# Turning the normalised activations between sublayers: a scaled copy and plain transposes in place of a product with a diagonal

## The chip, the cores and the metric

The kernel runs on one NeuronCore of a Trainium2 chip. The metric is the device time of one execution in microseconds (us). TensorE does the matrix products, VectorE, ScalarE and GpSimd work on tiles, SyncE issues the DMAs. In the rows they are PE (PEld its weight loads), DVE, ACT, POOL and SP.

## The reference

One step of a two-layer backbone over 512 latent and 128 context tokens, width 1024, all in float32. Each layer has three sublayers, FFN, mixing, FFN; each takes a normalised and modulated copy of the running tokens `x` and adds its gated result to it:

```python
def rmsnorm(x, g):
    y = xf * lax.rsqrt(jnp.mean(xf * xf, axis=-1, keepdims=True) + EPS)
    return (y * g.astype(jnp.float32)).astype(x.dtype)

def modulate_in(x, g_pre, mod, j):
    return rmsnorm(x, g_pre) * (1.0 + mod[:, :, 3 * j + 1]) + mod[:, :, 3 * j]

def gated_residual(x, out, g_post, mod, j, weight):
    return x + weight * mod[:, :, 3 * j + 2] * rmsnorm(out, g_post)
```

The mixing is neighbourhood attention and mLSTM heads in layer 0, a gated short convolution in layer 1. The products are done as three products of rounded high and low parts (`hT_hi`, `hT_lo`, `w_hi`, `w_lo`), 320 or 512 columns each.

## The kernel before

The 640 tokens are five tiles of 128 (`NT` = 5), held in SBUF for the whole run as `X`, tokens on the partitions, 1024 columns a tile. The six sublayers (`SUBS`) follow one another; `boundary(s)` of ScalarE and VectorE, the tile loops of GpSimd and `turn_x(s)` of TensorE are the stretch between sublayer s-1 and s. Each engine runs its own instructions in program order, and semaphores tie them together. No scheduler has a part in it: the order is that of the code.

For each tile the boundary does this, the steps of one tile interleaved with those of its neighbours:

- VectorE evacuates the output sums from PSUM (`evac`, L1267), gates the second half (L1245), and adds the result to `X` (`add_out`, L1250) once GpSimd has the factor of the output's norm (`post_r`, L1119 and L1120).
- ScalarE squares the new tile and sums it (`square_x`, L920).
- GpSimd makes the row factor 1/rms of it (`pre_r`: L1103, L1104) and multiplies it into a diagonal 128x128 matrix (L1127). Two diagonals exist. GpSimd's order is post_r(q), pre_r(q-1), for q = 0 to 5.
- TensorE turns the tile: eight float32 products with a slice of `X` as the stationary operand and the diagonal as the moving one (L607), which scales the rows and puts the features on the partitions. They go to one of two PSUM areas `TR` (banks 6 and 7, or 4 and 5).
- ScalarE modulates, which is a scale and a bias per feature (`modulate`, L930, eight activations), and VectorE splits the result into high and low parts (`split_h`, L1255 and L1256).

`first_units` then starts the next sublayer's products (L614): the first half of the columns needs tiles 0 to 2, the second half all five (`hT_ready`). They come after all of `turn_x` in TensorE's order. The first boundary (s = 0) has no output to add. ScalarE splits the second weight tile after modulating tile 3, VectorE after splitting tile 3.

Of the kernel before, what the change touches and what calls it, by code (L numbers as in the profile page):

```python
# [20 lines left out]
ALU = mybir.AluOpType  # L21
ACT = mybir.ActivationFunctionType
AX = mybir.AxisListType
P = 128

D = 1024
LAT, CTX = 512, 128
TOK = LAT + CTX
NT = TOK // P
CT = LAT // P  # L30
KD = D // P
# [89 lines left out]
def build(nc, x_prompt, x_sample, cache_k, cache_v, state_C, state_n, state_m, c, c_ctx, ada_w,  # L121
# [4 lines left out]
    with ctx:  # L126
        sb = lambda name, shape, dt=F32: ctx.enter_context(nc.sbuf_tensor(name, shape, dt))
        sem = lambda name: ctx.enter_context(nc.semaphore(name))
        at = lambda name, shape, off, dt=F32: nc.alloc_sbuf_tensor_at(name, shape, dt, offset=off)
# [4 lines left out]
        end = nc.sbuf_usable_end  # L134
        o = base

        def take(name, shape, dt=F32):
            nonlocal o
            t = at(name, shape, o, dt)
            size = 4  # L140
            for w in shape[1:]:
                size *= w
            where[name] = o
            o += (size + 31) // 32 * 32
            return t

        where = {}
        X = take("x", [P, NT, D])
# [10 lines left out]
        ident = take("ident", [P, P])  # L159
# [5 lines left out]
        ssq = take("mean_sq", [P, 3, NT])  # L165
        msq = take("mean_sq_eps", [P, 3, NT])
        rms = take("rms", [P, 2, NT])
        diag = take("diag", [P, 2, P])
        ones = take("ones", [P, 1])
        halfneg = take("minus_half", [P, 20])  # L170
        ccol = take("cond_cols", [P, 2, KD])
# [16 lines left out]
        assert conv_at + 2 * (TOK + 16) * 4 <= end  # L188

        h_mod = at("h_mod", [P, 2, KD, P], arena)  # L190

        ada0 = at("ada_first", [P, PRO, KD, MODW], arena)
        adab0 = at("ada_bias_first", [2, PRO * MODW], where["part"])
# [59 lines left out]
        TR = [flat(pair(6)).rearrange("p (k t) -> p k t", t=P), flat(pair(4)).rearrange("p (k t) -> p k t", t=P)]  # L253
# [12 lines left out]
        act_ready, out_ready, out_evac = sem("act_ready"), sem("out_ready"), sem("out_evac")  # L266
        ssq_post, r_post, x_new = sem("ssq_post"), sem("r_post"), sem("x_new")
        ssq_half, gated_half, gated = sem("ssq_half"), sem("gated_half"), sem("gated")
        ssq_pre, diag_ok, xT_ok = sem("ssq_pre"), sem("diag_ok"), sem("xT_ok")
        hmod_ok, hT_ready = sem("hmod_ok"), sem("hT_ready")  # L270
        s_dve, s_pool = sem("s_dve"), sem("s_pool")
        s_ident, s_const, s_slow, s_x, s_c = sem("s_ident"), sem("s_const"), sem("s_slow"), sem("s_x"), sem("s_c")
# [289 lines left out]
        def _(pe):  # L562
            mm = nc.tensor.matmul
# [3 lines left out]
            for i in range(PRO):  # L567
                for k in range(KD):
                    if k % (KD // 2) == 0:
                        pe.wait_ge(first_loaded[i][k // (KD // 2)], 16)  # L570
                    last = mm(PS[0:2, i, :], csil[:, :, k], ada0[:, i, k, :], start=(k == 0), stop=(k == KD - 1))
# [4 lines left out]
            for kind in range(2):  # L576
                for k in range(KD):
                    col = (kind * KD + k) * 2
                    last = nc.tensor.transpose(PS[:, 0, col:col + 2], flat(mrow0[:])[:, kind * D + k:(kind + 1) * D:KD], ident[0:2, 0:2])
# [15 lines left out]
            def turn_x(s):  # L595

                if s == 0:
                    pe.wait_ge(s_x, 32)
                    pe.wait_ge(neg_ok, 2)
                for t in range(NT):  # L600
                    pe.wait_ge(diag_ok, NT * s + t + 1)
                    if s and t < 2:
                        pe.wait_ge(out_evac, plan[s][0]["oe"] - (0 if t else NT))
                    if t >= 2:
                        pe.wait_ge(hmod_ok, NT * s + t - 1)
                    for k in range(KD):
                        last = mm(TR[t % 2][:, k, :], X[:, t, k::KD], diag[:, t % 2, :], start=True, stop=True)  # L607
                    last.then_inc(xT_ok, 1)

            def unit_half(p, h, width=P):  # L610
# [483 lines left out]
        @block.gpsimd  # L1094
        def _(pool):
            own = Steps(pool, s_pool)
            pool.memset(halfneg[:], -0.5).then_inc(neg_ok, 1)
            pool.memset(ones[:], 1.0).then_inc(neg_ok, 1)
            pool.wait_ge(neg_ok, 2)
            pool.wait_ge(s_ident, 16)  # L1100

            def rsqrt(dst, tmp, src, width, scale):
                own.link(pool.tensor_scalar(tmp, src, scale, EPS, ALU.mult, ALU.add))  # L1103
                return pool.tensor_tensor(dst, tmp, halfneg[:, 0:width], ALU.pow)  # L1104

            def gate_first_half(s, t):

                pool.wait_ge(ssq_half, NT * s + t + 1)
                if t == 0:
                    pool.wait_ge(gate_ready, s + 1)  # L1110
                if s:
                    pool.wait_ge(r_post, NT * s)
                pool.tensor_scalar(msq[:, 0, t:t + 1], ssq[:, 0, t:t + 1], EPS, None, ALU.add)  # L1113
                pool.tensor_tensor(part[:, t, 0:512], part[:, t, 0:512], G[:, cond(t), 0:512], ALU.mult).then_inc(gated_half, 1)

            def post_r(s, t):
                pool.wait_ge(ssq_post, NT * s + t + 1)
                pool.wait_ge(gated_half, NT * (s + 1))
                own.link(pool.tensor_tensor(msq[:, 1, t:t + 1], ssq[:, 1, t:t + 1], msq[:, 0, t:t + 1], ALU.add))  # L1119
                pool.tensor_tensor(rms[:, 1, t:t + 1], msq[:, 1, t:t + 1], halfneg[:, 0:1], ALU.pow).then_inc(r_post, 1)  # L1120

            def pre_r(s, t):
                pool.wait_ge(ssq_pre, NT * s + t + 1)
                own.link(rsqrt(rms[:, 0, t:t + 1], msq[:, 2, t:t + 1], ssq[:, 2, t:t + 1], 1, 1.0))
                if t >= 2:
                    pool.wait_ge(xT_ok, NT * s + t - 1)
                pool.tensor_scalar(diag[:, t % 2, :], ident[:], rms[:, 0, t:t + 1], None, ALU.mult).then_inc(diag_ok, 1)  # L1127

            for s, kind in enumerate(SUBS):
                for q in range(NT + 1):  # L1130
                    if s and q < NT:
                        post_r(s - 1, q)
                    if q:
                        pre_r(s, q - 1)
                if kind == "sc":
                    pool.wait_ge(hT_ready, NT * (s + 1))
                    pool.memset(upad[:], 0.0).then_inc(conv_zero, 1)
                if kind == "ab":
                    pool.wait_ge(hT_ready, NT * (s + 1))
                    pool.memset(padsb[:], 0.0).then_inc(pad_zero, 1)  # L1140
                    pool.memset(vmt[:, :, :, MLD:MLD + 1], 1.0).then_inc(ones_ok, 1)
                    pool.wait_ge(ones_ok, 1)
                    nv, nd = 0, 0
                    whole = [z[1] for q, z in enumerate(ML_STEPS) if z[1] in [y[1] for y in ML_STEPS[:q]]]

                    def head_r(n):
                        pool.wait_ge(h_ssq_ok, n + 1)
                        c4 = slice(whole[n] * MLH, (whole[n] + 1) * MLH)
                        rsqrt(hr[:, c4], hms[:, c4], hssq[:, c4], MLH, 1.0 / MLD).then_inc(h_r_ok, 1)

                    for q, (dr, cc) in enumerate(ML_STEPS):
                        edge = P - 1 if dr == 0 else 0
                        if cc < CT:
                            pool.wait_ge(ml_wi, q + 1)
                            if q >= 2:
                                pool.wait_ge(ml_num, q - 1)
                            pool.tensor_tensor(qs[:, q % 2], FT[:, 8:12, cc * P:(cc + 1) * P], wi[:, q % 2], ALU.mult).then_inc(ml_qs, 1)
                        if q in NEEDS_STATE:
                            pool.wait_ge(ml_w, q + 1)
                            if nv >= 2:  # L1160
                                pool.wait_ge(ml_c, nv - 1)
                            wl = Wx[:, q % 2, :, edge:edge + 1].to_broadcast([P, MLH, MLD + 1])
                            pool.tensor_tensor(vw[:, nv % 2], vmt[:, cc], wl, ALU.mult).then_inc(ml_vw, 1)
                            nv += 1
                        if cc in [z[1] for z in ML_STEPS[:q]]:
                            nd += 1
                            if nd >= 2:
                                head_r(nd - 2)
                    head_r(NT - 1)
                for t in range(NT):  # L1170
                    gate_first_half(s, t)
            for t in range(NT):
                post_r(len(SUBS) - 1, t)
# [515 lines left out]
```

## Time and profile before

| what | value |
|---|---|
| median of 3 runs | 3026.76 us (3025.64 to 3029.79) |
| span of the profiled execution | 3024.5 us |
| TensorE matmul busy | 2856.1 us (94%) |
| VectorE busy | 1460.8 us (48%) |
| ScalarE busy | 676.4 us (22%) |
| GpSimd busy | 188.8 us (6%) |
| mean granted clock of TensorE | 0.938 of full |
| L607, the turning products | 480 rows, 117.6 us busy |
| TensorE waiting for L1127 before L607 | 44.8 us |

The span reaches from the first instruction to the last; the page has no second figure for the profiled execution's time, so the span stands beside the runs. A float32 product appears as two rows of TensorE, two passes each. Rows of one engine that overlap are pipelined: the spacing of starts is what a product costs in a row of them, not its own length.

### The profile page before, as it was taken

Reading aid. Unit: us, or ns where it says so; the run is one execution under the profiler, and the core shown is the slowest. Engines: PE = TensorE matmul, PEld = TensorE weight load, DVE = VectorE, ACT = ScalarE, POOL = GpSimd, SP = SyncE. Lnnn points to the kernel's source line nnn. Section 1 sums busy time; section 2 is a strip of 40 time slices with the busy share of each in tenths; the row PEclk is TensorE's granted clock in tenths of the full one; section 3 lists DMA queues with packets and bytes.
Section 4 is the critical chain, followed back from the end, with each engine's and each line's share of the span. In section 5 each row is a group of like instructions: output and inputs, shape, how many; then the busy total and the mean of one; then the engine's idle time right before and its main releaser. Section 6 shows DMA issues by size and latency. Waiting matters only on the chain.

```text
span 3024.5 us, 42142 instructions
## 1 busy us (share of the span) xinstructions
PE 2856.1 (94%) x15952; PEld 2551.4 (84%) x15952; DVE 1460.8 (48%) x2590; ACT 676.4 (22%) x1192; POOL 188.8 (6%) x245
## 2 busy tenths in 40 slices
PE   8999999799979978899999989999999998999998
PEld 5997898599857766798899779889979998998996
DVE  2774774622155554675477367633334444322333
ACT  3111111322122121411111241111123114111212
POOL 1000000400000021200000120000012003000002
PEclk9999999999955578999999989999999999999999
DMA  5443443222510003343344224332221221222222
GB/s 198 139 125 105 139 139 119 77 70 70 94 37 19 7 7 88 92 138 97 112 138 150 81 86 138 107 94 76 87 80 50 77 87 54 75 66 84 73 87 87
DMA packets 384157, 276.06 MB, mean 91 GB/s; under 512 B 48224, under 2 KB 349728, under 8 KB 384052
## 3 DMA queue, kind: packets, MB, share of 16 engines
q1 hardware_dynamic: 384054, 274.67, 30.8%
q8 instruction: 67, 1.10, 0.2%
q14 instruction: 36, 0.29, 0.0%
HBM read 266.88 MB, written 7.71 MB: 91 GB/s over the span
## 4 chain that ended last, share of the span: by engine, by line
PE 56%; DVE 3%; POOL 1%; ACT 1%; issue 1%; DMA 0%; POOLq 0%; ACTq 0%; DVEq 0%
PE psum L645 35%; PE psum L591 6%; PE psum L592 6%; PE psum L593 6%; PE psum L614 2%; PE psum L607 2%; PE psum L587 1%; DVE w_lo L1225 1%; DVE mod_acc L1203 0%; ACT w_hi L897 0%; DVE part L1269 0%; DVE part L1267 0%; POOL rms L1104 0%; DVE gate L1241 0%; ACT h_mod L930 0%
## 5 line engine op out<-in xcount | busy, mean ns | idle before, releaser
L1225 DVE TENSOR_TENSOR w_lo<-w_raw,w_hi 128x1024 fp32r<-128x1024 f32 (+1 forms) x437 | 423.9, 970 | 1016.1 <-ACT w_hi L897 1010.9
L645 PE MATMUL psum<-hT_hi,w_hi 128*128 128x320 f32 (+1 forms) x3472 | 799.3, 311 | 4.2 <-DVE part L1269 4.2
L645 PE MATMUL psum<-hT_lo,w_hi 128*128 128x320 f32 (+1 forms) x3472 | 793.0, 310 | 0.0
L645 PE MATMUL psum<-hT_hi,w_lo 128*128 128x320 f32 (+1 forms) x3472 | 792.7, 309 | 0.0
L897 ACT ACTIVATE w_hi<-w_raw 128x1024 fp32r<-128x1024 f32 (+1 forms) x437 | 372.3, 852 | 1225.9 <-PE psum L593 537.8
L645 PEld LDWEIGHTS psum<-hT_hi,w_hi 128*128 128x128 f32 (+1 forms) x3472 | 579.3, 188 | 51.8 <-issue 45.1
L645 PEld LDWEIGHTS psum<-hT_lo,w_hi 128*128 128x128 f32 (+1 forms) x3472 | 581.3, 188 | 0.8
L645 PEld LDWEIGHTS psum<-hT_hi,w_lo 128*128 128x128 f32 (+1 forms) x3472 | 581.0, 188 | 0.8
L591 PE MATMUL psum<-w_hi,act_hi 128*128 128x512 f32 x960 | 382.9, 399 | 17.8 <-DVE mod_row L1214 9.7
L592 PE MATMUL psum<-w_lo,act_hi 128*128 128x512 f32 x960 | 380.2, 396 | 0.0
L593 PE MATMUL psum<-w_hi,act_lo 128*128 128x512 f32 x960 | 380.1, 396 | 0.0
L1203 DVE SCALAR_TENSOR_TENSOR mod_acc<-ada_raw,cond_silu,mod_acc 128x256 f32<-128x256 f32 x896 | 371.0, 482 | 0.0
L591 PEld LDWEIGHTS psum<-w_hi,act_hi 128*128 128x128 f32 x960 | 180.8, 188 | 78.7 <-DVE mod_row L1214 14.4
L593 PEld LDWEIGHTS psum<-w_hi,act_lo 128*128 128x128 f32 x960 | 180.8, 188 | 43.7
L592 PEld LDWEIGHTS psum<-w_lo,act_hi 128*128 128x128 f32 x960 | 180.7, 188 | 42.3
L968 ACT ACTIVATE silu_g<-psum 128x640 f32<-128x640 f32 x88 | 61.9, 704 | 613.8 <-PE psum L645 584.5
L1331 DVE TENSOR_TENSOR u_tmp<-psum,silu_g 128x640 f32<-128x640 f32 x88 | 72.6, 825 | 197.2 <-PE psum L645 195.8
L607 PE MATMUL psum<-diag,x 128*128 128x128 f32 x480 | 117.6, 420 | 44.8 <-POOL diag L1127 44.8
L607 PEld LDWEIGHTS psum<-diag,x 128*128 128x128 f32 x480 | 115.5, 335 | 47.9 <-POOL diag L1127 47.2
L1113 POOL TENSOR_SCALAR mean_sq_eps<-mean_sq 128x1 f32<-128x1 f32 x30 | 10.8, 360 | 2144.6 <-ACT junk L909 2144.4
L930 ACT ACTIVATE h_mod<-psum,mod_cols 128x128 f32<-128x128 f32 x240 | 87.7, 498 | 18.0 <-PE psum L607 18.0
L1314 DVE TENSOR_TENSOR act_lo<-u_tmp,act_hi 128x640 f32 (+1 forms) x96 | 79.3, 826 | 10.0
(170 smaller groups left out, 2034.8 us busy)
## 6 DMA issues: line engine op xcount, KB each, us to landing
w_raw<-in_ffn_w_dram SPq DMA_DIRECT2D x176, 512.0 KB, 4.1
ada_raw<-in_ada_w_dram SPq DMA_DIRECT2D x128, 512.0 KB, 3.6
w_raw<-in_ffn_w_dram SPq DMA_DIRECT2D x176, 256.0 KB, 2.6
w_raw<-in_ab_w_in_dram SPq DMA_DIRECT2D x28, 512.0 KB, 4.0
w_raw<-in_sc_w_in_dram SPq DMA_DIRECT2D x24, 512.0 KB, 4.0
ada_first<-in_ada_w_dram SPq DMA_DIRECT2D x8, 1024.0 KB, 12.6
gate<-modulation SPq DMA_DIRECT2D x6, 1024.0 KB, 6.1
w_raw<-in_ab_w_out_dram SPq DMA_DIRECT2D x16, 256.0 KB, 2.8
```

The lines of the kernel that those rows point to most:

```text
L591: mm(out, a_hi, b_hi, start=first, stop=False)
L592: mm(out, a_hi, b_lo, start=False, stop=False)
L593: return mm(out, a_lo, b_hi, start=False, stop=final)
L607: last = mm(TR[t % 2][:, k, :], X[:, t, k::KD], diag[:, t % 2, :], start=True, stop=True)
L645: last = mm(IN[p][0:width, h, 0:HT], a, b[:, k, h * HT:(h + 1) * HT], start=(k == 0 and a is hi and b is hT_hi), stop=(k == KD - 1 and a i ...
L897: A(dst, src, ACT.Copy).then_inc(w_hi_ok, 1)
L930: last = A(h_mod[:, t % 2, k, :], TR[t % 2][:, k, :], ACT.Identity, scale=mcol[:, s % 2, 1, cond(t), k:k + 1], bias=mcol[:, s % 2, 0, cond ...
L968: A(halves(sg[:]), IN_V[nb % 2], ACT.Silu).then_inc(in_evac[nb % 2], 1)
L1203: ins = V.scalar_tensor_tensor(acc[:, cd, :], w, col, acc[:, cd, :], ALU.mult, ALU.add)
L1225: V.tensor_tensor(d_, a, b.bitcast(F32), ALU.subtract).then_inc(w_lo_ok, 1)
L1314: V.tensor_tensor(lo, src, hi.bitcast(F32), ALU.subtract).then_inc(act_ready, 1)
L1331: V.tensor_tensor(halves(ut[:]), IN_V[p], halves(sg[:]), ALU.mult).then_inc(in_evac[p], 1)
```

## The change

The diagonals go. GpSimd multiplies the whole tile of `X` by its row factor into a new buffer `x_norm` of three tiles at the end of SBUF, and TensorE turns it with transposes against the identity matrix. The products' operands `X` and the diagonal are replaced; semaphore `diag_ok` becomes `xn_ok`; GpSimd may now run three tiles ahead of TensorE in place of two.

```diff
-        diag = take("diag", [P, 2, P])
...
+        xn = at("x_norm", [P, 3, D], (end - 3 * D * 4) // 32 * 32)
...
                 for t in range(NT):
-                    pe.wait_ge(diag_ok, NT * s + t + 1)
+                    pe.wait_ge(xn_ok, NT * s + t + 1)
...
                     for k in range(KD):
-                        last = mm(TR[t % 2][:, k, :], X[:, t, k::KD], diag[:, t % 2, :], start=True, stop=True)
+                        last = nc.tensor.transpose(TR[t % 2][:, k, :], xn[:, t % 3, k::KD], ident[:])
...
-                if t >= 2:
-                    pool.wait_ge(xT_ok, NT * s + t - 1)
-                pool.tensor_scalar(diag[:, t % 2, :], ident[:], rms[:, 0, t:t + 1], None, ALU.mult).then_inc(diag_ok, 1)
+                if t >= 3:
+                    pool.wait_ge(xT_ok, NT * s + t - 2)
+                pool.tensor_scalar(xn[:, t % 3, :], X[:, t, :], rms[:, 0, t:t + 1], None, ALU.mult).then_inc(xn_ok, 1)
```

## Rows read from the trace of the kernel before

**Rows 1.** The page, part 4: share of the chain that ended last, by line

```profile
PE psum L645 35%; PE psum L591 6%; PE psum L592 6%; PE psum L593 6%; PE psum L614 2%; PE psum L607 2%; PE psum L587 1%; DVE w_lo L1225 1%; DVE mod_acc L1203 0%; ACT w_hi L897 0%; DVE part L1269 0%; DVE part L1267 0%; POOL rms L1104 0%; DVE gate L1241 0%; ACT h_mod L930 0%
```

**Rows 2.** Timeline, TensorE, 2262:2291; start us, us, engine, line, operation, count, [idle before]

```profile
2270.49 11.74 PE L607 MATMUL psum<-diag,x 128*128 128x128 f32 x48 [7.37 <-POOL diag L1127]
2283.12 7.90 PE L607 MATMUL psum<-diag,x 128*128 128x128 f32 x32 [0.89 <-POOL diag L1127]
2290.77 0.39 PE L614 MATMUL psum<-hT_hi,w_hi 128*128 128x320 f32 x1
```

**Rows 3.** Timeline, GpSimd, 2263:2286

```profile
2267.48 0.19 POOL L1103 TENSOR_SCALAR mean_sq_eps<-mean_sq 128x1 f32<-128x1 f32 x1 [0.86 <-ACT part L920]
...
2269.25 1.18 POOL L1127 TENSOR_SCALAR diag<-ident,rms 128x128 f32<-128x128 f32 x1
...
2276.99 0.61 POOL L1127 TENSOR_SCALAR diag<-ident,rms 128x128 f32<-128x128 f32 x1
2278.20 0.19 POOL L1119 TENSOR_TENSOR mean_sq_eps<-mean_sq,mean_sq_eps 128x1 f32<-128x1 f32 x1 [0.61 <-ACT junk L909]
...
2284.74 0.61 POOL L1127 TENSOR_SCALAR diag<-ident,rms 128x128 f32<-128x128 f32 x1
```

**Rows 4.** Timeline, VectorE, 2255:2302

```profile
2269.26 0.68 DVE L1245 TENSOR_TENSOR part<-part,gate 128x512 f32<-128x512 f32 x1
...
2286.54 1.22 DVE L1256 TENSOR_TENSOR hT_lo<-h_mod,hT_hi 128x1024 fp32r<-128x1024 f32 x1
```

**Rows 5.** Timeline, TensorE, 1049:1056: transposes in the mixing stage

```profile
1049.28 2.40 PE L791 MATMUL psum<-ident,attn_tok 128*128 128x128 f32 x10
```

**Rows 6.** Timeline, TensorE, 680:683: transposes between weight products

```profile
680.27 0.71 PE L699 MATMUL psum<-ident,feat_tmp 128*128 128x128 f32 x5
```

**Rows 7.** Groups by line and form, GpSimd; busy us, mean ns, idle before

```profile
L1114 POOL TENSOR_TENSOR part<-part,gate 128x512 f32<-128x512 f32 x30 | 39.4, 1314 | 1.9
...
L1163 POOL TENSOR_TENSOR v_weighted<-vm_tok,decay 128x516 f32<-128x516 f32 x8 | 8.4, 1051 | 10.8 <-ACT decay L1076 10.8
...
L1137 POOL MEMSET u_pad<- 128x643 f32 x1 | 0.6, 636 | 10.7 <-DVE hT_lo L1256 10.7
...
L1097 POOL MEMSET minus_half<- 128x20 f32 x1 | 0.1, 114 | 0.3 <-POOLq L1677 0.3
```

**Rows 8.** Timelines, GpSimd and VectorE, 1056:1100: the mLSTM stage

```profile
1063.34 1.06 POOL L1163 TENSOR_TENSOR v_weighted<-vm_tok,decay 128x516 f32<-128x516 f32 x1
...
1064.10 0.85 DVE L1558 TENSOR_TENSOR decay<-decay,mlmask 128x512 f32<-128x512 f32 x1
```

**Rows 9.** Stretches; busy of each engine (x instructions), granted clock, DMA share, GB/s

```profile
853.00:1040.00 187.00, 186.41 (x626) 142.04 (x627) 100.84 (x307) 40.12 (x144) 0.00 (x0) 0.50 0.07 15
1049.00:1055.00 6.00, 4.93 (x22) 4.10 (x22) 4.15 (x6) 0.00 (x0) 0.00 (x0) 0.50 0.00 0
2274.00:2282.00 8.00, 8.00 (x35) 8.00 (x34) 5.11 (x6) 7.39 (x21) 6.70 (x11) 1.00 0.00 0
2285.00:2287.00 2.00, 2.00 (x10) 2.00 (x10) 1.16 (x2) 0.78 (x3) 0.35 (x1) 0.50 0.00 0
```

**Rows 10.** Timeline, TensorE, 1156:1162: first products after the mLSTM stage

```profile
1157.06 0.63 PE L592 MATMUL psum<-w_lo,hT_hi 128*128 128x512 f32 x1
...
1160.90 0.52 PE L592 MATMUL psum<-w_lo,hT_hi 128*128 128x512 f32 x1
1161.26 0.39 PE L593 MATMUL psum<-w_hi,hT_lo 128*128 128x512 f32 x1
...
1161.73 0.39 PE L592 MATMUL psum<-w_lo,hT_hi 128*128 128x512 f32 x1
```

**Rows 11.** Timelines, TensorE 39:60 and GpSimd 0:60: the first boundary

```profile
40.08 19.29 PE L607 MATMUL psum<-diag,x 128*128 128x128 f32 x80 [0.72 <-POOL diag L1127]
59.13 0.39 PE L614 MATMUL psum<-hT_hi,w_hi 128*128 128x320 f32 x1
...
53.78 0.61 POOL L1127 TENSOR_SCALAR diag<-ident,rms 128x128 f32<-128x128 f32 x1
```

More of the change, by code:

```diff
@@ L268, in build @@
         ssq_half, gated_half, gated = sem("ssq_half"), sem("gated_half"), sem("gated")
-        ssq_pre, diag_ok, xT_ok = sem("ssq_pre"), sem("diag_ok"), sem("xT_ok")
+        ssq_pre, xn_ok, xT_ok = sem("ssq_pre"), sem("xn_ok"), sem("xT_ok")
         hmod_ok, hT_ready = sem("hmod_ok"), sem("hT_ready")
```

## The prediction

> **What bounds the kernel now.** I read the chain of waits first. TensorE holds it: the biggest piece is the weight products of L645, and the turning products of L607 hold 2% [rows 1]. The change touches only L607 and what feeds it, so the place to read is the stretch between two sublayers, of which there are six. I take the one at 2263 to 2291 us as the pattern; those at 580, 1214, 1748 and 2517 us have the same shape, and from the first turning product to the first unit the same length within 0.15 us. The timeline of TensorE there [rows 2] shows three turned tiles in 11.74 us, a wait of 0.89 us for GpSimd, two more tiles, and the first unit's product at 2290.77. From 2283.12 to 2290.77 are two tiles, 3.83 us each (16 passes of float32). Everything after 2290.77 follows TensorE, so a boundary is worth what that one start moves.
>
> The next question is how far behind TensorE the others are. GpSimd's timeline [rows 3] runs from 2267.48 to 2285.35 (2284.74 + 0.61) with one wait of 0.61 us between two of its instructions; the small rows that are not shown fill the rest without gaps. It makes its last diagonal only 5.42 us before the first unit begins. **GpSimd is nearly a second bound**, hidden by one and a half tiles of TensorE. The first three tiles' high and low parts, which the first products need, are ready at 2287.76 (2286.54 + 1.22) [rows 4], so that wait ends 3 us before it matters.
>
> **TensorE's part.** Each tile's 8 float32 products (16 passes) become 8 transposes. The trace has transposes of the same shape, 128x128 float32 against the identity: 10 in 2.40 us at half the full clock [rows 5] and 5 in 0.71 us at the full clock [rows 6]. A single one's own length is included in each, so the spacing is about 0.225 and 0.11 us, and 8 take 2.0 us or 1.05 us. I take 2.0, because TensorE will work in short bursts (next part but one). Per tile 1.8 us of 3.83 go. But of five tiles only the last one lies on the path after GpSimd's last row: the others vanish in waits for GpSimd. Their 7 us are worth nothing here.
>
> **GpSimd's part.** Five times per boundary the multiplication of 128 columns becomes one of 1024. Undisturbed it took 0.61 us before [rows 3]. No row has 1024 columns on this engine, so I bound it from slopes [rows 7]:
> - lowest: memsets of 20 and of 643 columns took 0.114 and 0.636 us, 0.84 ns a column, and 0.61 + 896 x 0.84 ns = 1.36 us.
> - the product with one streamed operand and one that is spread from a single column, 516 columns, 1.05 us: less 0.19 for the shortest instruction, 1.67 ns a column, and 0.61 + 896 x 1.67 ns = 2.11 us.
> - the product of two streamed operands, 512 columns, 1.31 us: 2.2 ns, so 2.58 us.
> - highest: 0.19 us for 1 column against 0.61 for 128 [rows 3] is 3.3 ns a column, so 3.57 us.
> I take 2.11 us: it is the row with the same kind of operands, one streamed tile times one value per partition. The ends stay for the range. The Trainium skill's page "GPSIMD Engine Reference", section "When to use GPSIMD", says otherwise: there such one-input work goes at roughly the line rate and only two-input work is about twice as slow as on VectorE (where it advises elementwise work to go). A line rate is what the memset row shows; the sum by it is the first rival.
>
> The five rows together grow by 5 x (2.11 - 0.61) = 7.5 us. Nothing covers them: GpSimd does not idle there, and its next r for the residual stands behind each scaling, so the addition to x of the later tiles, the square on ScalarE and again GpSimd's next factor all slide. The last scaling ends at 2285.35 + 7.5 = 2292.85, and 2.0 us of transposes end at 2294.9. The first unit starts 4.1 us later than 2290.77. Both the wait of 0.61 us, which may be absorbed, and the new collisions work on this figure, in opposite directions.
>
> **The collisions.** A GpSimd instruction that starts while VectorE works on two SBUF operands waits for it: a diagonal started at 2269.25 took 1.18 us instead of 0.61, and VectorE's gating product ran from 2269.26 for 0.68 us [rows 3, 4]. It works the other way as well: in the mLSTM stage VectorE's addition at 1064.10 took 0.85 us instead of 0.69 beside a GpSimd product that ended at 1064.40 [rows 8]. With scalings of 2 us VectorE will wait up to 2 us at some of its additions and splits. I price it at zero to 1 us per boundary and leave it to the range, since VectorE has gaps of 1 to 2 us there.
>
> **The clock.** Before, TensorE is busy from 2270.49 on with one short break, and its granted clock is 1.00 at 2274 to 2282, 0.50 (1.2 GHz) for a moment at 2285 to 2287, and full (2.4 GHz) again when the units begin [rows 9]; the turning products were as long at either level, so it cost nothing. In the new form TensorE idles 7 us and more, then works 2 us in every 5. In the stretch with bursts of transposes and short products, 853 to 1040 us, and in 1049 to 1055, the clock was 0.50 throughout [rows 9]. I expect 0.50 when the first unit begins. What that costs is seen after the mLSTM stage: dense products started at 1156.5, spaced 0.427 us until 1160.90 and 0.235 from 1161.26 on [rows 10]: ten products that each lose 0.19, **2.0 us** in 4.4 us. The same 4.4 us of half clock cost the L614 products the same share. That is 2.0 us for each of the five boundaries. Nothing covers it, TensorE having no slack from there on.
>
> **The first boundary** (at 40 us) has no residual ahead of it. There TensorE ran 19 us without a break and GpSimd waited for it; its last diagonal ran at 53.78, the first unit started at 59.13 [rows 11]. With 2.11 us in place of 0.61 that last scaling ends at 55.9, or 57.2 if it must wait for a split of VectorE, and the transposes at 57.9 to 59.2. That is 0 to 1.2 us earlier, against 0 to 2 us of clock: I count nothing.
>
> **The sum.** 5 x (4.1 + 2.0) + 0 = 30.5 us. The profiled span is 3024.5 us; the runs' median of 3026.76 is 2.3 us longer, which I take as work outside the span that stays. 3024.5 + 30.5 = 3055 of span, **3057 us** as a time.
>
> **The rivals.**
> 1. GpSimd at the memset's rate, 1.36 us. Then the last scaling ends at 2285.35 + 3.75 = 2289.1, the transposes at 2291.1, 0.3 us late. With the clock's 2.0 this gives 5 x 2.3 = 11.5 us, 3038; with a full clock 1.5 us, 3028. For it: nothing but the memset's slope. Against it: the 516-column row, and the 0.42 us that 127 more columns added to the smallest row of the same kind. Chance 0.15 (0.10 with little or none of the clock's loss, 0.05 with it). What the page says of one-input work is this rival.
> 2. **Faster.** The freed 1.8 us of TensorE's tile comes through. The point from which it decides is the length of a scaling: 2285.35 + 5 x (S - 0.61) + 2.0 = 2290.77 gives S = 1.29 us. At 1.1 us and with a full clock (transposes in 1.05 us) the units would start 1.9 us earlier, of which some 1.5 remain since the second weight tile's low part is not ready before; five times that and some 3 us at the first boundary, where each step waits for TensorE and the first tile would be done at 39.9 + 1.1 + 1.1 instead of 40.1 + 3.8, is 10.5 us: 3016. For it: TensorE was the last to finish in every boundary. Against it: 1.1 us is below all four bounds. Chance 0.11.
> 3. The scaling at the highest slope, 3.57 us, or at 2.58 with VectorE's additions waiting behind it. Late by 5 x 2.96 - 3.42 (5.42 less the 2.0 us of transposes) = 11.4 us, with the clock 13.4, five times 67 us, and the first boundary loses about 8: 3102; at 2.58 it is 5 x (6.4 + 2.0) = 42, 3069. Chance 0.14 for over 3075.
> 4. The forecast, a scaling of 1.7 to 2.6 us with a cold or half-cold clock: 3045 to 3070. Chance 0.60.
> That the change would not do what it says can be set aside: the diff leaves no diagonal, and both engines' instructions at L607 and L1127 are replaced one by one, none added.
>
> **How the numbers follow.** The range of 3026 to 3090 leaves out the faster case and the far end of rival 3, and holds rival 1 nearly whole. About 0.2% (6 us) is what a measurement of this kernel can tell from no change. Faster by more than that: rival 2, 0.11. Within: rival 1 without the full loss, 0.10. Slower: 0.60 + 0.14 + 0.05 = 0.79.
>
> **What the new profile would show.** The group of L1127 on GpSimd near 2.1 us undisturbed, up to 2.9 beside VectorE; TensorE's waits for it grown from 44.8 us to over 80 and spread over nearly every tile; L607 with 240 rows in place of 480 and about 55 us busy; the first L614 product of the pattern boundary some 4 us later after the last product before it; a granted clock of 0.50 at that product and a spacing near 0.27 us for about 4 us. A scaling below 1.3 us, or a full clock at the first unit, would make the prediction wrong.

## The result and the profile after

| | before | changed |
|---|---|---|
| median of the runs on this chip | 3026.2 us (4 runs, 3025.5 to 3029.8) | 3076.86 us (4 runs, 3075.4 to 3078.7) |
| ratio to before | 1 | 1.0163 (95% interval 1.0149 to 1.0178) |
| profiled span | 3024.5 us | 3073.6 us, +49.1 |
| mean granted clock of TensorE | 0.938 | 0.918 |
| TensorE waiting for L1127 before L607 | 44.8 us | 146.4 us |
| GpSimd busy | 188.8 us | 263.3 us, +74.5 |

The change makes the kernel 1.6% slower, some 50 us. The prediction said 3057 us with a range of 3026 to 3090; the direction and the place were right, the size was short by 20 us.

The page of the changed kernel, first the busy times of part 1, then the chain of part 4 (compare [rows 1]; this chain was followed back only over 15% of the span, so its shares can't be set beside the old ones):

```profile
PE 2802.3 (91%) x15712; PEld 2489.7 (81%) x15712; DVE 1465.6 (48%) x2590; ACT 677.5 (22%) x1192; POOL 263.3 (9%) x245
...
PE psum L645 10%; PE psum L591 2%; PE psum L593 2%; PE psum L592 2%; PE psum L614 0%; DVE part L1267 0%; DVE x L1250 0%; DVE w_lo L1225 0%; DVE gate L1241 0%; PE psum L607 0%; POOL mean_sq_eps L1119 0%; DVE part L1269 0%; ACT w_hi L897 0%; ACT junk L909 0%; DVE part L1245 0%; POOLq L126 0%
```

TensorE does 54 us less work and the kernel is 49 us longer. The groups by line (busy us, mean ns of one, then idle before and its releaser) say where the waiting is:

```profile
L607 PE MATMUL psum<-ident,x_norm 128*128 128x128 f32 x240 | 59.1, 426 | 146.4 <-POOL x_norm L1127 146.4
```

```profile
L1127 POOL TENSOR_SCALAR x_norm<-x,rms 128x1024 f32<-128x1024 f32 x30 | 103.2, 3439 | 3.1
```

```profile
L1250 DVE SCALAR_TENSOR_TENSOR x<-part,rms,x 128x1024 f32<-128x1024 f32 x30 | 38.6, 1286 | 57.3 <-POOL rms L1120 57.0
```

TensorE's wait grew by 102 us, more than the 58.5 us of turning work that went. One scaling costs 3.44 us on average, where the prediction took 2.11. VectorE's addition of the residual, L1250, waits 57 us for GpSimd's row factor (20 before).

The pattern boundary on TensorE, as in [rows 2] (start us, us, line, count, idle before). Here the last product ahead of it starts at 2292.13:

```profile
2302.14 1.97 PE L607 MATMUL psum<-ident,x_norm 128*128 128x128 f32 x8 [9.61 <-POOL x_norm L1127]
2308.23 1.97 PE L607 MATMUL psum<-ident,x_norm 128*128 128x128 f32 x8 [4.13 <-POOL x_norm L1127]
2315.52 1.97 PE L607 MATMUL psum<-ident,x_norm 128*128 128x128 f32 x8 [5.31 <-POOL x_norm L1127]
2322.28 1.97 PE L607 MATMUL psum<-ident,x_norm 128*128 128x128 f32 x8 [4.79 <-POOL x_norm L1127]
2327.46 1.97 PE L607 MATMUL psum<-ident,x_norm 128*128 128x128 f32 x8 [3.21 <-POOL x_norm L1127]
2329.09 0.62 PE L614 MATMUL psum<-hT_hi,w_hi 128*128 128x320 f32 x1
2329.50 0.47 PE L614 MATMUL psum<-hT_lo,w_hi 128*128 128x320 f32 x1
...
2331.97 0.31 PE L614 MATMUL psum<-hT_hi,w_lo 128*128 128x320 f32 x1
```

Every tile is waited for, 3.2 to 5.3 us each, and each is turned in 1.97 us. Before, the first unit's product came 27.66 us after the end of the last weight product; now it comes 36.57 us after it, 8.9 us later. In the five boundaries it is 7.1, 8.8, 8.8, 8.9 and 8.8 us later, 42.3 us in all. That is most of the 49.1.

GpSimd in the same stretch, as in [rows 3]:

```profile
2296.89 0.19 POOL L1103 TENSOR_SCALAR mean_sq_eps<-mean_sq 128x1 f32<-128x1 f32 x1 [0.86 <-ACT part L920]
...
2298.66 3.42 POOL L1127 TENSOR_SCALAR x_norm<-x,rms 128x1024 f32<-128x1024 f32 x1
...
2304.78 3.40 POOL L1127 TENSOR_SCALAR x_norm<-x,rms 128x1024 f32<-128x1024 f32 x1
...
2309.33 1.67 POOL L1104 TENSOR_TENSOR rms<-mean_sq_eps,minus_half 128x1 f32<-128x1 f32 x1
2311.11 4.36 POOL L1127 TENSOR_SCALAR x_norm<-x,rms 128x1024 f32<-128x1024 f32 x1
...
2318.39 3.84 POOL L1127 TENSOR_SCALAR x_norm<-x,rms 128x1024 f32<-128x1024 f32 x1
...
2324.56 2.85 POOL L1127 TENSOR_SCALAR x_norm<-x,rms 128x1024 f32<-128x1024 f32 x1
```

It works without a gap from 2296.89 to 2327.41, and the first unit starts 1.68 us after that: the last tile's transposes start at 2327.46, and the unit's product follows in the spacing of starts, 1.63 us later (1.97 us is the length of the row, with the last transpose's own end in it). The last scaling, with nothing beside it, takes 2.85 us; the other four take 3.40 to 4.36. VectorE shows why, as in [rows 4]:

```profile
2298.68 0.67 DVE L1245 TENSOR_TENSOR part<-part,gate 128x512 f32<-128x512 f32 x1
2302.98 1.28 DVE L1250 SCALAR_TENSOR_TENSOR x<-part,rms,x 128x1024 f32<-128x1024 f32 x1 [3.63 <-POOL rms L1120]
...
2311.00 1.23 DVE L1256 TENSOR_TENSOR hT_lo<-h_mod,hT_hi 128x1024 fp32r<-128x1024 f32 x1
2312.14 0.68 DVE L1245 TENSOR_TENSOR part<-part,gate 128x512 f32<-128x512 f32 x1
...
2318.28 1.23 DVE L1256 TENSOR_TENSOR hT_lo<-h_mod,hT_hi 128x1024 fp32r<-128x1024 f32 x1
2321.65 1.13 DVE L1255 CAST hT_hi<-h_mod 128x1024 fp32r<-128x1024 f32 x1 [2.14 <-ACT h_mod L930]
```

The scaling issued at 2311.11 has VectorE's subtraction (two SBUF operands) in front of it from 2311.00, and the gating product right behind that, until 2312.82; it lasts 1.51 us longer than the undisturbed one. The one at 2304.78 meets one product of 0.68 and lasts 0.55 longer. Where the scaling is in front, VectorE pays: the cast at 2321.65 takes 1.13 in place of 0.69 us. GpSimd's small steps are lengthened as well: L1104 takes 0.57 us where nothing is beside it (at 2284.07 in the kernel before) and 1.39 to 1.67 us in all five tiles here. But in the kernel before four of five took 1.40 to 1.56, and all small steps together grow by only 0.1 us in this boundary, so this is no part of the loss.

The clock, by stretches as in [rows 9]:

```profile
2302.00:2308.00 6.00, 1.97 (x8) 1.57 (x8) 2.48 (x3) 3.70 (x10) 5.65 (x6) 0.50 0.00 0
2327.00:2329.00 2.00, 1.54 (x7) 1.54 (x8) 1.74 (x2) 1.14 (x2) 0.41 (x1) 0.50 0.00 0
2329.00:2331.00 2.00, 2.00 (x10) 2.00 (x9) 1.35 (x2) 1.52 (x5) 0.00 (x0) 0.50 0.00 0
2331.00:2333.00 2.00, 2.00 (x14) 2.00 (x13) 0.59 (x1) 1.38 (x4) 0.00 (x0) 0.83 0.55 146
2333.00:2336.00 3.00, 3.00 (x23) 3.00 (x22) 1.33 (x2) 0.00 (x0) 0.63 (x1) 1.00 0.26 78
```

The first unit meets a granted clock of 0.50 (1.2 GHz), and in the TensorE rows above its products start 0.267 us apart until 2331.6 and 0.147 from then on. Over what a unit loses before too, that adds 1.14 us in the first boundary and 0.51, 0.52, 0.57, 1.16 and 0.84 in the others.

The first boundary, as in [rows 11]:

```profile
57.64 1.97 PE L607 MATMUL psum<-ident,x_norm 128*128 128x128 f32 x8 [1.90 <-POOL x_norm L1127]
59.26 0.61 PE L614 MATMUL psum<-hT_hi,w_hi 128*128 128x320 f32 x1
```

```profile
54.73 2.85 POOL L1127 TENSOR_SCALAR x_norm<-x,rms 128x1024 f32<-128x1024 f32 x1
```

Its first unit starts at 59.26 in place of 59.13. GpSimd is the bound there too now, and ends just as late as TensorE had. The clock's 1.14 us does not arrive: the stretch from this unit to the next boundary's last weight product is only 0.1 us longer than before.

The account of 49.1 us, from the ends of the weight products and the starts of the units: 42.3 us in the five boundaries, 0.1 in the first, 3.6 of slow first products in the five, and 3.1 left over. This rest lies in the stretch between the second and the third boundary (608.12 us in place of 604.42, of which 0.5 is clock), where the wait of L739 for VectorE is 14.8 us in place of 12.9. The same stretch was 605.0 to 607.4 us long in the experiments, in no order with what they change, so the changed kernel's is the longest of all; its cause stays open.

### The profile page after: what moved, and what is told of

Its sections match the earlier page's. It is cut to its first block and busy times, and to the rows that moved or that the text cites. A ratio compares the mean times of both kernels' runs of the same rounds, so it can differ in the third digit from the quotient of the medians.

```text
span 3073.6 us, 41656 instructions
## 1 busy us (share of the span) xinstructions
PE 2802.3 (91%) x15712; PEld 2489.7 (81%) x15712; DVE 1465.6 (48%) x2590; ACT 677.5 (22%) x1192; POOL 263.3 (9%) x245
## 5 line engine op out<-in xcount | busy, mean ns | idle before, releaser
L592 PEld LDWEIGHTS psum<-w_lo,act_hi 128*128 128x128 f32 x960 | 181.0, 189 | 42.4
L607 PE MATMUL psum<-ident,x_norm 128*128 128x128 f32 x240 | 59.1, 426 | 146.4 <-POOL x_norm L1127 146.4
L607 PEld LDWEIGHTS psum<-ident,x_norm 128*128 128x128 f32 x240 | 47.1, 220 | 158.3 <-POOL x_norm L1127 155.2
L1127 POOL TENSOR_SCALAR x_norm<-x,rms 128x1024 f32<-128x1024 f32 x30 | 103.2, 3439 | 3.1
L930 ACT ACTIVATE h_mod<-psum,mod_cols 128x128 f32<-128x128 f32 x240 | 86.7, 465 | 26.1 <-PE psum L607 26.0
```

The source lines that it names most:

```text
L592: mm(out, a_hi, b_lo, start=False, stop=False)
L607: last = nc.tensor.transpose(TR[t % 2][:, k, :], xn[:, t % 3, k::KD], ident[:])
L930: last = A(h_mod[:, t % 2, k, :], TR[t % 2][:, k, :], ACT.Identity, scale=mcol[:, s % 2, 1, cond(t), k:k + 1], bias=mcol[:, s % 2, 0, cond ...
L1127: pool.tensor_scalar(xn[:, t % 3, :], X[:, t, :], rms[:, 0, t:t + 1], None, ALU.mult).then_inc(xn_ok, 1)
```

## The experiments

Two theories stand at the start. Theory A is the prediction's, with GpSimd's length corrected: the boundary is as long as GpSimd's chain, and a first unit is later by the growth of five scalings less TensorE's old lead of 3.4 us; the clock is a small second term. Rivals put the loss on the transposes, on the cold clock, or on the waits between VectorE and GpSimd.

### 1 and 2. The scaling cut to 128 and to 512 columns

The tile is turned from x itself, so the scaling of the rows is missing from these kernels' results; from one to the other only the length of GpSimd's instruction changes.

```diff
-                        last = nc.tensor.transpose(TR[t % 2][:, k, :], xn[:, t % 3, k::KD], ident[:])
+                        last = nc.tensor.transpose(TR[t % 2][:, k, :], X[:, t, k::KD], ident[:])
...
-                pool.tensor_scalar(xn[:, t % 3, :], X[:, t, :], rms[:, 0, t:t + 1], None, ALU.mult).then_inc(xn_ok, 1)
+                pool.tensor_scalar(xn[:, t % 3, 0:128], X[:, t, 0:128], rms[:, 0, t:t + 1], None, ALU.mult).then_inc(xn_ok, 1)
```

The second has 0:512 in place of 0:128.

> The transposes stay, but GpSimd scales only the first 128 columns of a tile (0.61 us, as the diagonal took), and TensorE turns x itself. The scaling of the rows is left out. Theory A, GpSimd's chain sets the start of the next sublayer: 5 x 2.24 us of scaling and its collisions go from each boundary, the first unit starts up to 3.4 us earlier than in the kernel before in boundaries 1 to 5 (2 to 2.5 us of it kept, the second weight tile's low part being next), about 4 us earlier in the first, less 0.5 to 1.2 us of clock each: a span of 3010 to 3018 us against 3024.5 before. Theory B, the short bursts of transposes and the half clock behind them are the cost: it stays over 3050.

> As e1, with 512 columns scaled. The line through 0.61 us for 128 and 2.85 us for 1024 columns gives 1.57 us for a scaling. Theory A: the first unit is 5 x 0.96 - 3.42 = 1.4 us later than before in boundaries 1 to 5, and with 0.8 us of clock each and 1.5 us gained at the first the span is about 3034 us (3030 to 3040). If not a line but a threshold is behind the loss (one scaling shorter than TensorE's old tile of 3.8 us is hidden), this kernel is as fast as e1.

128 columns: 3011.85 us, ratio 0.9947 (0.9931 to 0.9964), span 3010.8, **13.7 us faster than before**. 512 columns: 3041.7 us, ratio 1.0047 (1.0030 to 1.0064), span 3042.4. Both kernels' L1127 groups, and from the second a scaling in the first boundary, where nothing is beside it:

```profile
L1127 POOL TENSOR_SCALAR x_norm<-x,rms 128x128 f32<-128x128 f32 x30 | 37.4, 1246 | 3.1
```

```profile
L1127 POOL TENSOR_SCALAR x_norm<-x,rms 128x512 f32<-128x512 f32 x30 | 70.2, 2341 | 3.1
```

```profile
41.68 1.57 POOL L1127 TENSOR_SCALAR x_norm<-x,rms 128x512 f32<-128x512 f32 x1
```

So an undisturbed scaling takes 0.61, 1.57 and 2.85 us at 128, 512 and 1024 columns: exactly 2.5 ns per column on top of 0.29 us. The transposes are the same in all three kernels, which clears them: with short scalings they win 13.7 us. In the last four boundaries first units come 2.6 to 2.7 us later than before at 512 columns, 1.3 in the first of the five (the prediction's formula, 5 x (1.57 - 0.61) - 3.42, gives 1.4; in the pattern boundary the five scalings together run 4.6 us over their undisturbed length, 1.6 before), and 3.0 to 3.9 us earlier at 128 columns (formula: 3.42 earlier). The first was inside its expectation, the second some 2 us above: the formula holds to about 1 us per boundary, collisions come on top. A straight line between the two spans crosses 3024.5 at 1.03 us of scaling, about 300 columns; the prediction put the break-even of the first units at 1.29 us, with no loss of clock behind them.

### 3. The change with float32 products in place of the transposes

```diff
-                        last = nc.tensor.transpose(TR[t % 2][:, k, :], xn[:, t % 3, k::KD], ident[:])
+                        last = mm(TR[t % 2][:, k, :], xn[:, t % 3, k::KD], ident[:], start=True, stop=True)
```

> The changed kernel, with float32 products against the identity in place of the transposes, so GpSimd's 1024 columns alone are left of the change; computes all. Theory A: of TensorE's five tiles only the last lies behind GpSimd's last row, so it is 1.9 us slower than the changed kernel in each of the six boundaries, less what a higher clock gives back (up to 0.8 each): a span of 3079 to 3086 us against 3073.6. Theory B, the transposes' bursts cost through the clock: it is faster than the changed kernel by 5 us or more.

3085.28 us, ratio 1.0191 (1.0174 to 1.0208), span 3083.8. As expected: the last tile's products are on the path behind GpSimd, and the first units come 2.1 to 2.3 us later than in the changed kernel (3.7 in the first boundary): a tile of products takes 3.85 us up to the first unit's start there, the transposes 1.63. The transposes by themselves are worth about 10 us even where GpSimd is late (10.2 by the spans, 0.28% by the ratios).

### 4. The changed kernel with products in TensorE's waits

Before each turned tile of boundaries 1 to 5, TensorE runs products whose results are not used (24 before the first tile, 8 before each other).

```diff
+                    if s:
+                        if t == 0:
+                            pe.wait_ge(w_lo_ok, plan[s][0]["nin"] + 1)
+                            pe.wait_ge(out_evac, plan[s][0]["oe"] - NT)
+                        p = plan[s][0]["nin"] % 2
+                        for _ in range(24 if t == 0 else 8):
+                            mm(PS[:, 0, :], w_hi[:, p, 0, :], w_hi[:, p, 0:4, :].rearrange("p a b -> p (a b)"), start=True, stop=True)
```

> The changed kernel, with products nobody reads put into TensorE's idle time of boundaries 1 to 5: 24 of 512 columns before the first tile, 8 before each other, so that the clock stays up. Theory A: only what the trace of the changed kernel shows as slow first products comes back, 0.5 to 1.2 us per boundary and 0.9 us of each boundary's last transposes, together 5 to 8 us: a span of 3066 to 3069 us. Theory B: most of the 49 us comes back, under 3045.

3069.18 us, ratio 1.0147 (1.0130 to 1.0164), span 3065.9, 7.7 us under the changed kernel's; by the ratios the gain is 0.16%, and their intervals overlap. The number is where it was expected, but the trace backs only part of it. The first units come 0.2 to 0.7 us earlier (2.3 us in five boundaries, the last transposes being quicker). The slow first products vanish in boundaries 1 and 3 but not in 2, 4 and 5, where they lose 1.1, 1.4 and 1.1 us: 3.6 us in all, as much as without the fillers. Here is the fourth: its third, fourth and fifth tile (the added lines make L607 into L614 and L1127 into L1134), and stretches around its first unit, which starts at 2321.15:

```profile
2308.16 1.97 PE L614 MATMUL psum<-ident,x_norm 128*128 128x128 f32 x8 [4.30 <-POOL x_norm L1134]
...
2314.92 1.16 PE L614 MATMUL psum<-ident,x_norm 128*128 128x128 f32 x8 [1.38 <-POOL x_norm L1134]
...
2320.11 1.39 PE L614 MATMUL psum<-ident,x_norm 128*128 128x128 f32 x8 [2.18 <-POOL x_norm L1134]
```

```profile
2316.00:2320.00 4.00, 1.93 (x9) 1.24 (x7) 1.62 (x2) 3.85 (x9) 3.90 (x2) 1.00 0.00 0
2320.00:2323.00 3.00, 2.89 (x15) 2.89 (x16) 2.96 (x3) 1.46 (x5) 0.06 (x1) 0.65 0.00 0
2323.00:2326.00 3.00, 3.00 (x18) 3.00 (x17) 1.49 (x2) 1.44 (x5) 0.00 (x0) 0.78 0.51 140
```

The fillers don't fill the waits: TensorE still idled 4.30, 1.38 and 2.18 us before the third, fourth and fifth tile. The granted clock was 1.00 at 2316 to 2320, where TensorE was busy 1.93 of 4 us, and then 0.65 and 0.78, where it was busy nearly all the time. So this run does not show what a TensorE that never idles would be granted. Of the rest of the 7.7 us, 3.1 lie in the stretch between the second and the third boundary, 0.5 of them slow products and the others the length that scatters in all kernels. What these fillers gave back by quicker transposes and products is 2 to 3 us of the 49. The rival that most of the loss is the clock's falls; a full clock at the first unit is not had reliably by these fillers.

### 5. The scaling on VectorE

GpSimd keeps the row factor and hands it over; VectorE scales behind its addition for the tile after. Transposes as in the change.

```diff
-                own.link(rsqrt(rms[:, 0, t:t + 1], msq[:, 2, t:t + 1], ssq[:, 2, t:t + 1], 1, 1.0))
-                if t >= 3:
-                    pool.wait_ge(xT_ok, NT * s + t - 2)
-                pool.tensor_scalar(xn[:, t % 3, :], X[:, t, :], rms[:, 0, t:t + 1], None, ALU.mult).then_inc(xn_ok, 1)
+                rsqrt(rms[:, 0, t:t + 1], msq[:, 2, t:t + 1], ssq[:, 2, t:t + 1], 1, 1.0).then_inc(r_pre, 1)
...
+            def scale_x(s, t):
+                dve.wait_ge(r_pre, NT * s + t + 1)
+                if t >= 3:
+                    dve.wait_ge(xT_ok, NT * s + t - 2)
+                V.tensor_scalar(xn[:, t % 3, :], X[:, t, :], rms[:, 0, t:t + 1], None, ALU.mult).then_inc(xn_ok, 1)
...
+                    if 2 <= q < NT + 2 and s < len(SUBS):
+                        scale_x(s, q - 2)
```

> The scaling goes from GpSimd to VectorE, behind its addition to the tile after (x_norm of tile q - 2 after add_out of tile q - 1); the transposes stay; computes all. VectorE's cast of 1024 columns took 0.69 us, so a scaling should take 0.7 (1.2 if it runs at one column a cycle). Theory A: GpSimd's chain loses even the diagonal, so TensorE's 1.8 us per tile finally count: the first unit starts 2 to 3.4 us earlier than before in boundaries 1 to 5, 3 to 4 us in the first, less 0.5 to 1.2 us of clock each: a span of 3010 to 3017 us, faster than both kernels. Rival: VectorE's own order (it now waits for GpSimd's factor with additions and splits queued behind it) takes what it gives, and the span is 3022 to 3035 us.

3013.06 us against 3030.27 of the kernel before on that chip, ratio 0.9946 (0.9932 to 0.9959), span 3008.9. **It computes everything and beats both kernels**: 0.5% faster than before, 2.1% faster than the change as it was made. The VectorE group and, from the pattern boundary, ScalarE's and TensorE's rows at its end:

```profile
L1253 DVE TENSOR_SCALAR x_norm<-x,rms 128x1024 f32<-128x1024 f32 x30 | 22.6, 752 | 11.1 <-POOL rms L1104 11.0
```

```profile
2271.46 5.67 ACT L930 ACTIVATE h_mod<-psum,mod_cols 128x128 f32<-128x128 f32 x16
```

```profile
2271.09 1.97 PE L607 MATMUL psum<-ident,x_norm 128*128 128x128 f32 x8 [2.48 <-DVE x_norm L1253]
2274.48 1.94 PE L607 MATMUL psum<-ident,x_norm 128*128 128x128 f32 x8 [1.42 <-ACT h_mod L930]
2276.42 0.60 PE L614 MATMUL psum<-hT_hi,w_hi 128*128 128x320 f32 x1
```

The same 1024 columns that take GpSimd 2.85 us take VectorE 0.75. The first units come 3.6 to 3.8 us earlier than before, 4.4 in the first boundary. GpSimd's part of the chain is no longer last, if only just: the fifth tile waits for ScalarE's modulated copies (h_mod, L930), which run back to back, and its scaling on VectorE had ended 0.38 us before the transposes start (2274.10 and 2274.48). Of 22.8 us won at the first units, 7.8 are given back by slower first products (0.75 to 2.1 us in each boundary where before had 0.3); TensorE still works in bursts.

### 6. The same with products in TensorE's waits

The fillers of run 4 (4 in place of 8 before the later tiles) on top of run 5.

> e4 with products nobody reads before the tiles of boundaries 1 to 5, 24 before the first and 4 before each other. If the clock is what e4 still loses, the first products run at the full level and it is 3 to 6 us faster than e4; if the fillers stand in the way of the tiles, it is no faster or slower.

3011.93 us, ratio 0.9941 (0.9927 to 0.9954), span 3010.2. No difference that can be told from run 5's 0.9946. The slow first products are gone in three of the five boundaries that have fillers (0.66 us where run 5 loses 0.75, 2.1 and 0.9), but what is left there is a wait for the second weight tile's low part; in the other two, and in the first boundary, which has none, they still lose 1.7 to 2.0 us. A negative result: fillers are not worth their code here.

### 7. VectorE's scaling with float32 products

Run 5 with run 3's edit, the fourth corner of the square.

> e4 (row scaling on VectorE) with TensorE turning the scaled tile by eight float32 products with an identity instead of eight transposes; all of the computation is kept. Theory A (transposes pay only where the chain ahead of TensorE is short): with the scaling 0.75 us on VectorE the tiles are ready sooner than TensorE can turn them by products, so TensorE is the bound again at 5 tiles x 3.83 us; the first unit comes about as in the kernel before, +27 to +29 us after the last product ahead of the boundary (24.5 in e4), and the profiled span is 3017 to 3026 us, 8 to 17 us above e4's 3008.9. Rival B (TensorE's work in the boundary never matters, only the tiles' arrival does): the span is that of e4, 3007 to 3012 us.

3021.76 us (10 runs) against 3027.08 (13), ratio 0.9983 (0.9974 to 0.9993); the profiled execution was the longest of the ten, with a span of 3025.4, so the comparison goes by the ratio: 0.37% of 3027, or 11 us, above run 5. TensorE in the pattern boundary:

```profile
2276.93 7.85 PE L607 MATMUL psum<-ident,x_norm 128*128 128x128 f32 x32 [0.31 <-DVE part L1270]
2284.93 7.88 PE L607 MATMUL psum<-ident,x_norm 128*128 128x128 f32 x32 [0.15 <-DVE x_norm L1253]
2292.56 0.39 PE L614 MATMUL psum<-hT_hi,w_hi 128*128 128x320 f32 x1
```

TensorE is the bound again from the second tile on, with waits of 0.31 and 0.15 us only, and the first unit comes 26.9 us after the last weight product (27.7 before, 24.1 in run 5), at the edge of the 27 to 29 expected. Theory A holds for this kernel. But with run 3 beside it, its heading "transposes pay only where the chain ahead of TensorE is short" is refuted: in ratios, transposes for products give 0.28% (1.0191 to 1.0163) with the late chain and 0.37% with the short one, which the intervals can't tell apart. At the first units the short chain does get more, 2.8 to 2.9 us in each of the five boundaries in place of 2.1 to 2.3, and the colder clock takes some of it back: the first products are at full speed in all six boundaries of this run and slow in all six of run 5. The place of the scaling moves six to eight times as much (1.0163 against 0.9946).

### 8. GpSimd's order changed

All instructions are those of the change; the scaling is issued one iteration later, directly behind the residual's row factor and ahead of the next tile's own factor.

```diff
-                own.link(rsqrt(rms[:, 0, t:t + 1], msq[:, 2, t:t + 1], ssq[:, 2, t:t + 1], 1, 1.0))
+                own.mark(rsqrt(rms[:, 0, t:t + 1], msq[:, 2, t:t + 1], ssq[:, 2, t:t + 1], 1, 1.0))
...
-                for q in range(NT + 1):
+                for q in range(NT + 2):
...
-                    if q:
-                        pre_r(s, q - 1)
+                    if q >= 2:
+                        scale_x(s, q - 2)
+                    if 1 <= q <= NT:
+                        factor(s, q - 1)
```

> The changed kernel with GpSimd's order altered: each scaling is issued one iteration later, behind the row factor's last step of the tile after, so that this step never waits behind a scaling; all of the computation is kept. Theory A (GpSimd is simply full: 5 scalings and 5 sets of small steps and additions in a row): the order changes nothing in the sum, the profiled span stays at 3069 to 3080 us (3073.6 in the changed kernel). Rival B (what costs is the queue: small steps that VectorE's next work needs stand behind a scaling of 2.85 us): the boundaries get shorter by at least 2 us each, and the span is 3063 us or less.

3058.8 us, ratio 1.0112 (1.0095 to 1.0129), span 3056.3: **17.3 us less than the changed kernel from order alone** (0.51%, some 15 us, by the ratios). The first units come 2.0 us earlier than in the changed kernel in the first of the five boundaries and 3.6 in each of the others, 16.5 in all. That is on rival B's side of the line, and A's "the order changes nothing" is refuted. But the trace shows a third mechanism. GpSimd's group, its rows in the pattern boundary, and VectorE's addition there:

```profile
L1130 POOL TENSOR_SCALAR x_norm<-x,rms 128x1024 f32<-128x1024 f32 x30 | 85.5, 2851 | 1.6
```

```profile
2290.00 2.86 POOL L1130 TENSOR_SCALAR x_norm<-x,rms 128x1024 f32<-128x1024 f32 x1
...
2300.82 2.85 POOL L1130 TENSOR_SCALAR x_norm<-x,rms 128x1024 f32<-128x1024 f32 x1
2303.74 0.51 POOL L1103 TENSOR_SCALAR mean_sq_eps<-mean_sq 128x1 f32<-128x1 f32 x1
2304.33 1.56 POOL L1104 TENSOR_TENSOR rms<-mean_sq_eps,minus_half 128x1 f32<-128x1 f32 x1
2306.00 2.85 POOL L1130 TENSOR_SCALAR x_norm<-x,rms 128x1024 f32<-128x1024 f32 x1
...
2311.18 2.85 POOL L1130 TENSOR_SCALAR x_norm<-x,rms 128x1024 f32<-128x1024 f32 x1
```

```profile
2290.11 2.08 DVE L1255 SCALAR_TENSOR_TENSOR x<-part,rms,x 128x1024 f32<-128x1024 f32 x1 [0.51 <-POOL rms L1120]
```

GpSimd is still full from the first scaling to the last, as A has it. What shrank is its own work: every one of the 30 scalings takes 2.85 us, where the change's took 3.44 on average, 17.7 us less in sum; the small steps grow a little, and its rows at L1103, L1104, L1119, L1120 and the scaling sum to 171.8 us where they summed to 187.0. In the change, GpSimd releases VectorE's residual addition with L1120, does two small steps, and starts the scaling some 2 us later, when the addition is over and VectorE's next work on SBUF has just begun or begins with it (2311.00 and 2311.11 in the rows above); here the scaling starts first, in the same moment as the factor releases the addition, and VectorE pays instead: its addition takes 2.08 us in place of 1.28 at 2290.11. VectorE has the room. So collisions were not a matter of 0 to 1 us per boundary; some 3 us per boundary were to be had by which of the two starts first.

## Why the prediction was right, and where it was short

**The bound, and the lateness as the currency.** Right. The first unit's start decides, and 42.4 of the 49.1 us are the differences of those starts.

**"Of five tiles only the last one lies on the path."** Right: TensorE waits for every tile, and run 3 shows one tile's saving arriving, 2.1 to 2.3 us per boundary. That is 3.85 less the 1.63 between the starts of the last tile and of the first unit, not the 1.86 of 3.83 less 1.97.

**Transposes, 2.0 us a tile.** Right as a length, 1.97, and 0.3 us too long as what stands between the last scaling and the first unit (1.68).

**The scaling, 2.11 us.** This is the term that was mis-sized: 2.85 us undisturbed. The 516-column row was the nearest in kind and its 1.67 ns a column was still wrong; the two bounds on either side of 2.85 were the product of two streamed tiles (2.58) and the slope between 1 and 128 columns (3.57). No row of the trace before gives the slope; runs 1 and 2 measured it, 2.5 ns, and with it the instruction's own 0.61 us at 128 columns gives all three points. In the sum, 5 x (2.85 - 2.11) is 3.7 us per boundary, 18.5 in five.

The Trainium skill's page "GPSIMD Engine Reference", section "When to use GPSIMD", calls one-input work there roughly line rate. The measurement disagrees for this instruction: 2.5 ns a column, near the 2.2 of the two-operand product [rows 7] and far from the memset's 0.84, and 3.8 times VectorE's 0.75 us for the same tile. Its advice to put elementwise work on VectorE is what run 5 confirms.

**Collisions, "zero to 1 us per boundary".** Too low, and left out of the sum. In the pattern boundary the four disturbed scalings lose 3.6 us in place of 1.6 before, against a gap of 0.6 us that was absorbed. With the corrected scaling the formula gives 5 x 2.24 - 3.42 = 7.8; measured 8.9. The remaining 1.1 us is 2.0 of collisions and 0.1 of small steps, less the absorbed 0.6 and the 0.3 by which the last transposes hold the unit back less. (The first of the five boundaries has 7.1 us, 0.7 less than the formula.)

**The clock, 2.0 us per boundary.** Right in kind, granted 0.50 at the first unit in all six, and wrong in size: 0.5 to 1.2 us, 3.6 in five boundaries in place of 10. The analogy [rows 10] had 4.4 us of slow products behind a long stretch at 0.50; here the full clock came 1 to 2.5 us after the first product. The whole difference of the spans from the predicted 30.5 us is then +21.8 for the lateness (18.5 of it the scaling's length, 3.3 the collisions less the absorbed gaps and the shorter hand-over), -6.4 for the clock, +0.1 for the first boundary and +3.1 left open, together 18.6. The clock's price, nearly three times too high, hid part of the miss: with 3.6 us in its place the forecast would have been 3051, some 26 us short.

**The first boundary, nothing.** Right in the number, 0.1 us, and partly by luck: the last scaling ended at 57.58, outside the predicted 55.9 to 57.2, the unit followed 1.68 us behind it in place of 2.0, and the clock's 1.14 us did not arrive.

**The rivals.** Rival 1, the memset's rate, and rival 2, faster, fall with the measured 2.85 us; but run 1 is rival 2's mechanism made true, though with half the full clock at most of its first units, and it gained 13.7 us with a scaling of 0.61, where the rival had 10.5 for 1.1. The price of rival 3 at 2.58 us (3069) was nearest to the result, with a clock of 10 us in it that was not there; the case over 3075 had a chance of 0.14.

## What to carry to other kernels

An engine that finishes 5 us ahead of the bound in a 28 us stretch is not spare: before work is moved onto it, multiply the growth of its instruction by its count in the stretch and compare with the lead. Then ask for the same instruction's cost on the other engines: here VectorE did it in a quarter of the time and turned +1.6% into -0.5%. And where VectorE and GpSimd alternate over SBUF, the order of issue is itself a knob, worth 15 to 17 us here without removing an instruction.

## What the runs showed that was not expected

- GpSimd's product of a float32 tile with one value per partition is linear in its columns: 0.29 us + 2.5 ns each.
- The waits between VectorE and GpSimd are not symmetric. A scaling behind VectorE's two-operand work waits for nearly all of it (3.40 to 4.36 us in place of 2.85: 1.51 us more with 1.71 us of VectorE's work in front). VectorE's residual addition issued 0.11 us behind a scaling of 2.86 us takes 2.08 in place of 1.28: it loses 0.8 us, not the whole 2.75. A cast issued 0.58 us before the end of a scaling in front of it loses 0.44. The Trainium skill's page "SBUF — State Buffer", section "Who interferes with whom", has the later one blocked until the earlier one is through; the scalings fit that, the cast roughly (0.44 of 0.58), the addition does not.
- Products put into TensorE's waits did not hold its clock: in run 4 it was granted 1.00 in four us with TensorE busy 1.93, behind waits of 4.30 and 1.38 us, and 0.65 in the next three with TensorE busy 2.89, behind one more wait of 2.18.
- A slow clock at the first unit of the first boundary cost 1.1 us there and nothing at the next boundary. What takes it up stays open.
